# Two adaLN gate groups summed on VectorE beside layer 0's projections, sum steps in two halves

## The reference, cut to what matters

```
for l in range(2):
    shift, scale, gate       = split(silu(c)     @ ada_w[l] + ada_b[l], 3)   # ada_w[l]: 2048 x 6144
    shift_c, scale_c, gate_c = split(silu(c_ctx) @ ada_w[l] + ada_b[l], 3)
    h  = rmsnorm(x,  norm_g[l]) * (1 + scale)   + shift
    hc = rmsnorm(xc, norm_g[l]) * (1 + scale_c) + shift_c
    q, k, v, u_pool, u_four, g = split(h @ w_in[l]);  the same for hc
    mixed = concat(attention(q, k, v), pool(u_pool), fourier(u_four)) * silu(g)
    x  = x  + gate   * (mixed @ w_out[l]);  the same for xc
```

## Time and profile before

| | us |
|---|---|
| median of 3 runs | 2336.55 (2335.84 to 2337.86) |
| the profiled execution | 2333.01 |
| its span, first to last instruction | 2331.2 |
| TensorE busy in the span | 2247.7 |
| VectorE busy | 1415.2 |
| mean granted TensorE clock | 0.988 |

### The profile page before, as it was taken

One profiled execution on the slowest core, in us unless ns is written; L12 is line 12 of the kernel. 1 busy time (PEld: TensorE's weight loads), 2 busy tenths in 40 slices (PEclk: granted clock), 3 DMA queues, 4 the chain that ended last, 5 costly groups with the idle time before them and its releaser, 6 DMA issues.

```text
span 2331.2 us, 30004 instructions
## 1 busy us (share of the span) xinstructions
PE 2247.7 (96%) x11739; PEld 1835.9 (79%) x11739; DVE 1415.2 (61%) x2216; ACT 1038.6 (45%) x1590; POOL 271.2 (12%) x326
## 2 busy tenths in 40 slices
PE   5899999999999999999999998999999999999998
PEld 2477777788788767678888887888888888888887
DVE  3354533377688364546777776677755777567764
ACT  2232333332322254445554565555544555345553
POOL 1001100000011122100021324111100111001111
PEclk8999999999999999999999999999999999999999
DMA  9974433356655475635565544666656665666653
GB/s 356 331 262 171 149 122 120 114 184 196 211 176 176 165 266 191 218 102 169 189 217 178 180 137 157 189 190 188 186 196 190 187 189 182 197 188 183 190 190 117
DMA packets 322428, 437.14 MB, mean 188 GB/s; under 512 B 13848, under 2 KB 220112, under 8 KB 321264
## 3 DMA queue, kind: packets, MB, share of 16 engines
q1 hardware_dynamic: 316800, 413.19, 54.6%
q0 software_dynamic: 3392, 16.90, 2.0%
q10 hardware_dynamic: 2096, 5.15, 0.6%
HBM read 428.89 MB, written 6.29 MB: 187 GB/s over the span
## 4 chain that ended last, share of the span: by engine, by line
PE 86%; DVE 5%; ACT 3%; DMA 2%; issue 2%; POOL 1%; SPq 0%; ACTq 0%; POOLq 0%; DVEq 0%
PE ps L1382 25%; PE ps L1383 12%; PE ps L1357 8%; PE ps L1359 8%; PE ps L1358 8%; PE ps L1377 5%; PE ps L1379 5%; PE ps L1378 5%; PE ps L1337 2%; DVE SPL L1839 2%; ACT SPL L1595 2%; PE ps L1438 1%; PE ps L1455 1%; DMA RAW<-in_w_in_dram 1%; DMA RAW<-in_ada_w_dram 1%
## 5 line engine op out<-in xcount | busy, mean ns | idle before, releaser
L1839 DVE TENSOR_TENSOR SPL<-RAW,SPL 128x1024 fp32r<-128x1024 f32 x592 | 749.0, 1268 | 537.2 <-ACT SPL L1595 534.8
L1382 PE MATMUL ps<-HS,SPL 128*128 128x512 f32 x2688 | 954.5, 399 | 11.0 <-DVE SPL L1839 8.1
L1595 ACT ACTIVATE SPL<-RAW 128x1024 fp32r<-128x1024 f32 x592 | 622.2, 1056 | 478.1 <-PE ps L1359 170.2
L1383 PE MATMUL ps<-HS,SPL 128*128 128x256 f32 x2688 | 754.0, 280 | 0.0
L1382 PEld LDWEIGHTS ps<-HS,SPL 128*128 128x128 f32 x2688 | 506.2, 188 | 134.9 <-DVE SPL L1839 5.7
L1383 PEld LDWEIGHTS ps<-HS,SPL 128*128 128x128 f32 x2688 | 509.1, 189 | 2.0 <-issue 1.7
L1357 PE MATMUL ps<-SPL,HS 128*128 128x512 f32 x960 | 396.8, 413 | 13.4 <-DVE SPL L1839 5.3
L1359 PE MATMUL ps<-SPL,HS 128*128 128x512 f32 x960 | 377.4, 393 | 0.0
L1358 PE MATMUL ps<-SPL,HS 128*128 128x512 f32 x960 | 376.9, 393 | 0.0
L1357 PEld LDWEIGHTS ps<-SPL,HS 128*128 128x128 f32 x960 | 182.2, 190 | 76.1 <-issue 17.3
L1358 PEld LDWEIGHTS ps<-SPL,HS 128*128 128x128 f32 x960 | 182.6, 190 | 41.5 <-issue 6.0
(11 more groups left out here) (291 smaller groups left out, 1834.6 us busy)
## 6 DMA issues: line engine op xcount, KB each, us to landing
RAW<-in_w_in_dram SPq DMA_DIRECT2D x208, 512.0 KB, 4.9
RAW<-in_ada_w_dram SPq DMA_DIRECT2D x192, 512.0 KB, 4.9
RAW<-in_ffn_w_up_dram SPq DMA_DIRECT2D x192, 512.0 KB, 3.6
RAW<-in_w_out_dram SPq DMA_DIRECT2D x96, 512.0 KB, 4.6
RAW<-in_ffn_w_down_dram SPq DMA_DIRECT2D x96, 512.0 KB, 4.2
x_spill<-XT POOLq DMA_DIRECT2D x2, 2048.0 KB, 14.3
XT<-x_spill POOLq DMA_DIRECT2D x1, 4096.0 KB, 13.0
MM<-in_x_dram ACTq DMA_DIRECT2D x2, 1024.0 KB, 11.4
```

The source lines that it names most:

```text
L1382: mm(PS[b][:, :], wr, hh, start=k == 0, stop=False, skip_group_check=True)
L1383: m = mm(PS[b][:, 256:512], wl, hh[:, 0:256], start=False, stop=k == KT - 1, skip_group_check=True)
L1595: act(SPL[:, (n - 1) % NSPL, 0, :], raw_of(i), ACT.Copy).then_inc(s_hi, 1)
L1839: tt(w[:, 1, :], raw_of(s["i"]), w[:, 0, :].bitcast(F32), ALU.subtract).then_inc(s_lo, 1)
```

## The change

Groups 10 and 11 of layer 0 are made by `ada_sums`, with two accumulators of their own in `MM` (`ACC[2]`, the ends of its two halves, which hold tokens of x at first and later outputs of the Fourier part). Their 16 chunks stand one after each even chunk from 0 to 30. The pairs of TensorE's adaLN chunks (groups 8 and 9 of layer 0, group 0 of layer 1) stand after chunks 3, 7, 11, ..., 39 and after 33 and 37. A sum step is now two steps of two instructions: the first is put when the chunk is taken, the second is kept in `later` and put before the second part of the chunk being multiplied, or else at the next call of `run_ahead`. This holds for the sums of layer 1 as well.

```diff
--- before.py
+++ after.py
@@ -125,6 +125,7 @@
         T = lambda slot: TMP[:, slot, :]
 
         ACC = [MM[:, 0:2048].rearrange("p (h v c) -> p h v c", h=2, v=2), XT[:, 5120:7168].rearrange("p (h v c) -> p h v c", h=2, v=2)]
+        ACC.append(MM[:, :].rearrange("p (h x) -> p h x", h=2)[:, :, 3072:4096].rearrange("p h (v c) -> p h v c", v=2))
         XR = MM[:, 0:2048].rearrange("p (k n) -> p k n", n=256)
         LR = MM[:, 2048:4096].rearrange("p (k n) -> p k n", n=256)
         LI = MM[:, 4096:6144].rearrange("p (k n) -> p k n", n=256)
@@ -234,7 +235,7 @@
         at = {"loaded": 0, "taken": 0, "split": 0, "used": 0, "pos": 0, "ahead": AHEAD, "multiplied": 0, "summed": 0}
         after_chunk, acc_last = {}, {}
         split_no, chunk_split = {}, {}
-        hi, low = [], []
+        hi, low, later = [], [], []
         need = {}
 
         def use(*banks):
@@ -275,6 +276,7 @@
                 at["loaded"] += 1
 
         def run_ahead():
+            flush(later)
             load_ahead()
             while at["taken"] < min(len(queue), at["pos"] + (START_AHEAD if at["pos"] < 72 else at["ahead"])):
                 i = at["taken"]
@@ -292,8 +294,11 @@
 
         def add_products(i, c):
             g = c.group
-            put("ada_sum", i=i, kc=c.kc, acc=g.acc, before=at["summed"], last=g.room() if c.kc == 0 else [])
-            at["summed"] += 2 * len(g.acc)
+            add = lambda kk, before, last: put("ada_sum", i=i, kc=c.kc, kk=kk, acc=g.acc, before=before, last=last)
+            add(0, at["summed"], g.room() if c.kc == 0 else [])
+            at["summed"] += len(g.acc)
+            later.append(lambda before=at["summed"]: add(1, before, []))
+            at["summed"] += len(g.acc)
             after_chunk[i] = (s_acc, at["summed"])
 
         def pop_side(n):
@@ -895,7 +901,7 @@
                 flush(low)
                 last = multiplied()
                 if both:
-                    put("back", last=[last, (s_accT, 3), (s_gm, KT), (s_gs, KT)])
+                    put("back", last=[last, (s_accT, 5), (s_gm, KT), (s_gs, KT)])
                     for k in range(KT):
                         put("m2", k=k, last=[gated[k], last])
                 need["out", l] = (lambda k: [(s_m2, k + 1)]) if both else (lambda k: [gated[k]])
@@ -1111,8 +1117,9 @@
         main0, outs0, (sq0,), x0, (front0, last_out0), project0 = layer(0)
         main1, outs1, (sq1, sq1f), x1, (begin_h1, begin1), project1 = layer(1)
         sq_gm, sq_lru, sq2 = Squares(2, 7), Squares(2, 7), Squares(2, KT - 1)
-        left = [c for g in range(8, 12) for c in ada_group(0, g)] + [c for g in (0, 7) for c in ada_group(1, g)]
+        left = [c for g in (8, 9) for c in ada_group(0, g)] + [c for g in (0, 7) for c in ada_group(1, g)]
         gates1 = [c for g in range(8, 12) for c in ada_group(1, g)]
+        sums_0 = [c for g in (10, 11) for c in ada_sums(0, g, 2, 2, lambda: [(s_turn, KT), (s_sqx, 4)])]
         sums_a = [c for g in (4, 1, 5) for c in ada_sums(1, g, 2, 1, lambda: [(s_fm, 4)])]
         sums_b = [c for g in (2, 6, 3) for c in ada_sums(1, g, 2, 0, lambda: [(s_m2, KT)])]
         marks = []
@@ -1121,7 +1128,15 @@
             chunks.extend(cs)
             marks.append(len(chunks))
 
-        lay_out(main0[0] + mixed(main0[1][:40], left) + [c for pair in zip(main0[1][40:], sums_a) for c in pair])
+        front = []
+        for i, c in enumerate(main0[1][:40]):
+            front.append(c)
+            if i < 32 and i % 2 == 0:
+                front.extend(sums_0[i // 2:i // 2 + 1])
+            if i % 4 == 3 or i > 32 and i % 4 == 1:
+                front.extend(left[:2])
+                del left[:2]
+        lay_out(main0[0] + front + [c for pair in zip(main0[1][40:], sums_a) for c in pair])
         lay_out(outs0[:4] + [c for pair in zip(outs0[4:], sums_b) for c in pair] + left[:4] + outs0[28:])
         del left[:4]
         lay_out(left[:FILL])
@@ -1877,19 +1892,18 @@
                         stt(S2[:, l, 4 * (g - 4):4 * (g - 3), :], a, 1.0, VV[:, c:c + 4].unsqueeze(2).to_broadcast([P, 4, 2]), ALU.add, ALU.mult).then_inc(s_s2, 1)
 
                 elif kind == "ada_sum":
-                    i, kc, vectors = s["i"], s["kc"], len(s["acc"])
+                    i, kc, kk, vectors = s["i"], s["kc"], s["kk"], len(s["acc"])
                     for sm, v in new((s_c, 1), *s["last"]):
                         e.wait_ge(sm, v)
                     e.wait_ge(s_raw[i % NRAW], 16 * (i // NRAW + 1))
-                    for kk in range(2):
-                        w = raw_of(i)[:, kk * 512:(kk + 1) * 512]
-                        for v, acc in enumerate(s["acc"]):
-                            c = CW[:, 4 * kc + 2 * kk + v:4 * kc + 2 * kk + v + 1]
-                            if kc == 0 and kk == 0:
-                                ts(acc, w, c, None, ALU.mult).then_inc(s_acc, 1)
-                            else:
-                                e.wait_ge(s_acc, s["before"] + vectors * (kk - 1) + v + 1)
-                                stt(acc, w, c, acc, ALU.mult, ALU.add).then_inc(s_acc, 1)
+                    w = raw_of(i)[:, kk * 512:(kk + 1) * 512]
+                    for v, acc in enumerate(s["acc"]):
+                        c = CW[:, 4 * kc + 2 * kk + v:4 * kc + 2 * kk + v + 1]
+                        if kc == 0 and kk == 0:
+                            ts(acc, w, c, None, ALU.mult).then_inc(s_acc, 1)
+                        else:
+                            e.wait_ge(s_acc, s["before"] + v + 1 - vectors)
+                            stt(acc, w, c, acc, ALU.mult, ALU.add).then_inc(s_acc, 1)
 
                 elif kind == "sum_turn":
                     l, g = s["l"], s["g"]
```

## The result

The changed kernel takes 2346.99 us (median of 5, 2346.17 to 2347.98), the kernel before, run beside it, 2335.84 (2331.12 to 2337.86): a ratio of 1.0053, 95% interval 1.0041 to 1.0066. It is slower by 11.2 us where 5.6 were forecast; the sign is right, the time lies above the range. The profiled execution of the changed kernel took 2346.17.

The account below looks back on a forecast made before the run. TensorE, busy 96% of the span, was taken to bound the kernel. -6.8 + 3.6 + 4.4 + 2.0 + 2.0 + 0.4 = +5.6 us on the median 2336.55 gave 2342.1, range 2338 to 2345.5.

Parts of the forecast that it names:

- TensorE's work: Layer 0 projection: 8 adaLN pairs (9.5 us) and two turns (0.9) removed, two sum turns (3.6) added: 6.8 us less.
- Key norms: Chunks 0 to 3: split and four multiply-adds delay the first reduction; TensorE waits 0.6, 2.7, 0.1, 0.2, sum 3.6 us.
- First query norms: Chunks 8 to 11: two splits and a half ahead of the reduction, another before the norm; waits taken as 4.4 us.
- The two rows behind: First query norms, after the first two rows: serial chain as long as TensorE's two steps, adding 0.4 us.
- The term for GpSimd's power: First query norms: a half may slow GpSimd's power as a split does, adding 0.9 us; 4.4 taken between 4.0 and 4.9.
- Second query norms: Chunks 16 to 19: early rows 0.25 us, last row 1.75 from a half and a held power; sum 2.0.
- Pool copy: Chunks 24 to 27: group 1's pool matrix copy behind six loads instead of four; 2.0 us, middle of 0 to 4.0.
- Second sum turn: End of chunk 31: runs before the last row copies, so the first Fourier matmul waits 0.4 us.
- The gate: Later stages: attention rows run two parts later, but the gates needing them come well after; 0 us.
- the third: Rival: attention rows late too, 1.5 us at four places, +11.6 us in all, 2348; chance 0.06.
- The first: Rival: no waits come at the three norm sequences, only TensorE's 6.8 us less count, 2329.8; chance 0.20.
- The signs named in the prediction: Matmul counts 512 and 128, waits at key and first query norms totalling 8 us, TensorE busy down some 7.

Follow-up runs that it names:

- the last run: Changed kernel with sums moved off the norms, pairs back inside them, 29 attention rows before the gate, second sum turn earlier: 2333.08 against 2336.93 us, ratio 0.9986.
- fewer pairs: Kernel before without 6 of the 8 adaLN pairs and with no sums in their place: median 3.8 us less than before, ratio 0.9978 to 0.9996.
- small sums: Changed kernel with 62 of the 64 multiply-adds cut to 8 of 512 columns: +4.2 us against before, ratio 1.0005 to 1.0028.
- keys step: Small sums with the one sum step ahead of the key norms back at full size: stage 459.0 us against 455.9, one execution, no median.
- whole sums: Changed kernel with each sum step's four multiply-adds together ahead of a chunk's first part: +14.2 us against before, ratio 1.0050 to 1.0085.
- rows kept: Changed kernel with attention rows run again in the parts ahead of each first-layer sum turn: +7.1 us against before, ratio 1.0026 to 1.0048.
- other orders: Changed kernel with sums moved off the norms (pool wait 3.49): +4.0 us against before; with the second group six chunks later (4.67): +5.8.
- the second execution: Changed kernel, unaltered, profiled and timed again: stage 462.8 us, median +9.2 us against before, ratio 1.0034 to 1.0058.
- before twice: Kernel before, unchanged, profiled two times: stage 453.9 and 453.1 us.
- the one with moved sums and rows restored: Changed kernel, sums off the norms, second group spread, pairs back, no attention row left out for group 8's turn: +0.5 us against before, ratio 0.9989 to 1.0008.

## Why the prediction was wrong

**TensorE's work: -6.8 forecast, -6.4 measured** in the last run, where no stretch at 1.2 GHz blurs it. From start to start the 64 matmuls of the pairs gave 8.0 us, with what stands behind them about 9.0 (1.12 a pair in the run with fewer pairs, not 1.19); the two turns 0.7, the two sum turns cost 3.5, which makes 6.2.

**Key norms: 3.6 forecast, 2.2 to 2.4 measured**, and 0.9 to 1.1 more for a late split a few us before in four other runs with this order there (small sums, keys step, whole sums, rows kept), where the forecast had 0.6. The step by step reading held: reduction at 157.38 (157.6 forecast), the normed row at 160.6 (160.8).

**First query norms: 4.4 forecast, 3.5 measured** (1.24 + 2.25, where 1.1 and 2.5 were said). The two rows behind cost nothing, 0.4 in the sum. The term for GpSimd's power, another 0.4, was too high as well: beside a half it took 1.45 us, not 1.91, with 1.01 when VectorE is idle. And it runs beside the half, which the norm has to wait for anyway: the half ends at 204.82, the norm starts at 205.05, so the power costs 0.2.

```profile
203.40 1.42 DVE L1906 SCALAR_TENSOR_TENSOR MM<-RAW,CW,MM 128x512 f32<-128x512 f32 x2
203.57 1.45 POOL L2346 TENSOR_TENSOR SM<-SM 128x4 f32<-128x4 f32 x1 [35.70 <-DVE SM L1961]
...
208.57 1.22 DVE L1854 TENSOR_TENSOR SPL<-RAW,SPL 128x1024 fp32r<-128x1024 f32 x1
208.74 1.91 POOL L2346 TENSOR_TENSOR SM<-SM 128x4 f32<-128x4 f32 x1 [3.72 <-DVE SM L1961]
...
214.38 1.01 POOL L2346 TENSOR_TENSOR SM<-SM 128x4 f32<-128x4 f32 x1 [3.73 <-DVE SM L1961]
```

The Trainium skill (SBUF — State Buffer, section Who interferes with whom) says that the two exclude each other for a whole instruction. An instruction of a half is 0.7 us long, a split 1.2, so the power's delays of 0.44 and 0.90 agree with it. The forecast's 0.9 for a half had taken the split's length.

**Second query norms: 2.0 forecast, 1.9 measured**, but 1.7 of it stands at the adaLN turn before, which the copy of an attention row held up (it stands behind a norm and a split on VectorE), and not at the transposes.

**Pool copy: 2.0 forecast, 0.4 measured** (0.2 with group 3, which waits 0.2 less than before). Five of the six loads stood ahead of the copy and one 0.7 us behind its issue, nearly as read. The price was wrong: two loads more made the time from issue to use 7.2 us instead of 6.9, and the wait 1.16 instead of 0.79. The waits of 3.49 and 4.67 in other orders are on another copy, that of group 3.

**Second sum turn: 0.4 forecast, 0.7 measured.**

**The gate: 0 forecast, 1.3 measured.** "The attention rows run two parts later" was seen and priced at nothing, since the gates come later: a term put at nothing without looking at a gate. What decides is not whether they are in time but which row then stands behind a gate, where VectorE's queue is 5.2 us deep. In the trace of before this wait was there to see, at 499 us.

**The clock: not in the forecast at all, 3.2 measured, 4.9 in the second execution.** This is the step that failed most: the sum takes every wait at its own length and has no term for the granted clock behind it. The added waits brought 6.8 us and, in the second execution, 10.2 us at 1.2 GHz, in which matmuls start 0.43 us apart for 0.23; from start to start each 3.4 us of it cost 1.6 to 1.8. That is most of the 4.0 us that TensorE's busy time lies above the last run's. The other 0.8 is an estimate: before a wait the last matmul's recorded 0.39 us counts as busy, while the next would start after 0.23, so 0.16 for each of the ten waits over 0.1 us in place of five.

The terms add up so: waits of 9.8 us where 12.4 were forecast, TensorE -6.4 for -6.8, together +3.4 in the stage, +4.2 with the 0.8; with the clock +7.4 to +9.0. That the forecast of +5.6 had the right sign and came as near as it did is in part luck: 2.6 us too much of waits stood in for a part of the clock. The medians lie higher still, +11.2 and +9.2; nothing outside the stage repeated between the two executions, and the cause of that rest stays open.

Of the rivals, the third (more waits, +11.6) has the number but not the mechanism: only the turn at 272 and the gate are attention rows, 3.0 us of added wait and not 6. The first, -6.8 with no waits, is what the best order comes near: -6.0 in the stage.

**The signs named in the prediction.** The matmuls of adaLN and the sum turn's are 64 fewer and 32 more, as said (512 and 128); the four waits near 158, 164, 205 and 210, together 8 us, came as 2.2 at 161, 1.2 at 208 and 2.2 at 214; TensorE's busy time did not fall by 7, which was the sign of the clock.

## What to carry to other kernels

Work moved to an engine that is idle on average is paid for at the places where its queue stands ahead of the engine that bounds: one 2.7 us step ahead of the key norms cost 3.1 us, and the same 40 us of work at other places, with the pairs put back between the norm steps, cost 0.4 us of idle time. Matmuls taken out from between such steps are cover taken away too: without any new work half of what was removed came back as waits. Before adding a wait to a TensorE-bound stage, price it with the clock: read whether waits of that size are followed by a slow stretch, and count the stretches as well as the waits.

## What the runs showed that was not expected

Stretches of 3.4 us at 1.2 GHz, or of 6.8, stand at added waits, and not at the same one each time: in after at 161.9 behind 2.23 us and at 503.2 behind 1.94 and within 0.88, but not at 213.6 behind 2.25; with small sums behind 2.2 at 211. The three executions with none of the sums' work or order (before twice, fewer pairs) and the last run have none in the stage, though fewer pairs has a wait of 2.08. The Trainium skill (Advanced Engine Details and Errata, section Clock Domains) says that the array's clock is gated to 1.2 GHz when it is idle. The runs agree as far as each of the stretches in the stage, in all 13 executions that have one, begins within a wait or at most 1.2 us behind its end. That one may also come with only 0.66 us of idle time is theirs alone: in five of the runs, as at 391 us in the one with moved sums and rows restored, behind the second sum turn, whose 16 matmuls have one column each.

```profile
387.00:391.00 4.00, 3.34 (x28) 2.40 (x27) 1.36 (x3) 1.70 (x3) 0.00 (x0) 1.00 0.05 7
391.00:394.40 3.40, 3.40 (x10) 2.64 (x9) 1.22 (x1) 1.04 (x2) 0.00 (x0) 0.50 0.93 311
```

What makes one such place fall into a slow stretch and the next not stays open, and so does whether the wait alone does it or what TensorE ran around it. It was not tried whether halves in the sums beside the gates, ahead of the row there, would shorten the gate's wait.
